# Down products as seven block products in place of eight: weight and activation quarters summed on the way, and one bank for the up products

## The reference

```python
def sq_relu_mlp(h, w_up, w_down):          # twice, D_FF = 4096
    return jnp.square(jax.nn.relu(h @ w_up)) @ w_down
# the FFN, D_FF_2 = 2816:  (silu(h @ w_gate) * (h @ w_up)) @ w_down
```

## Time and profile before

| | us |
|---|---|
| median of three executions (1137.82 to 1142.7) | 1138.17 |
| the profiled execution | 1141.42 |
| its span, first to last instruction | 1139.6 |
| TensorE busy in it | 1112.0 |
| VectorE busy | 707.6 |
| ScalarE busy | 583.6 |
| GpSimd busy | 142.6 |

### The profile page before, as it was taken

The page is one execution under the profiler, slowest core; times in us unless marked ns, Lnnn a source line. Parts: engine busy times, 40 slices in busy tenths (PEclk is TensorE's granted clock), DMA queues, the critical chain, the costliest instruction groups (busy, mean ns, idle before and its releaser), DMA issues.

```text
span 1139.6 us, 17781 instructions
## 1 busy us (share of the span) xinstructions
PE 1112.0 (98%) x7033; PEld 984.8 (86%) x7033; DVE 707.6 (62%) x997; ACT 583.6 (51%) x767; POOL 142.6 (13%) x105
## 2 busy tenths in 40 slices
PE   8899999999998999999999999999999999999997
PEld 7767888888887888888888999898899989999996
DVE  5764565565668646565656878566587566554554
ACT  5565544444579554444455546455555346443443
POOL 3543300000265240000030000000000011000001
PEclk9999999999999999999999999999999999999999
DMA  7917565555442236556545654436643545656552
GB/s 216 306 54 186 182 198 188 200 190 184 118 137 88 98 111 222 191 186 201 189 156 185 204 171 149 132 128 223 203 159 120 185 148 160 221 175 194 189 172 89
DMA packets 138782, 193.96 MB, mean 170 GB/s; under 512 B 7147, under 2 KB 112840, under 8 KB 138716
## 3 DMA queue, kind: packets, MB, share of 16 engines
q1 hardware_dynamic: 126796, 181.92, 48.4%
q10 hardware_dynamic: 11312, 11.05, 3.6%
q0 software_dynamic: 608, 0.08, 0.1%
HBM read 191.90 MB, written 6.37 MB: 174 GB/s over the span
## 4 chain that ended last, share of the span: by engine, by line
PE 83%; ACT 6%; DVE 5%; issue 2%; DMA 2%; POOL 0%; ACTq 0%; DVEq 0%; POOLq 0%
PE psum L548 20%; PE psum L549 20%; PE psum L550 20%; PE psum L709 11%; PE psum L710 5%; ACT arena L1552 3%; PE psum L637 2%; ACT whi L1566 2%; DVE wlo L2125 1%; DMA raw<-in_a_w_in 1%; PE psum L1264 1%; PE psum L668 1%; PE psum L1237 1%; DVE arena L2566 1%; DMA raw<-in_b_w_o 0%
## 5 line engine op out<-in xcount | busy, mean ns | idle before, releaser
L1566 ACT ACTIVATE whi<-raw 128x2048 fp32r<-128x2048 f32 (+2 forms) x174 | 325.9, 1875 | 255.5 <-PE psum L550 172.5
L2125 DVE TENSOR_TENSOR wlo<-raw,whi 128x2048 fp32r<-128x2048 f32 (+1 forms) x149 | 337.5, 2267 | 184.1 <-ACT whi L1566 183.2
L548 PE MATMUL psum<-xA,whi 128*128 128x256 f32 x840 | 239.8, 285 | 2.7 <-DVE wlo L2125 1.7
L549 PE MATMUL psum<-xA,whi 128*128 128x256 f32 x840 | 237.6, 283 | 0.0
L550 PE MATMUL psum<-xA,wlo 128*128 128x256 f32 x840 | 237.5, 283 | 0.0
L1535 POOL TENSOR_TENSOR wlo<-raw,whi 128x288 fp32r<-128x288 f32 (+3 forms) x56 | 112.6, 2037 | 793.8 <-ACT whi L1566 793.5
L709 PE MATMUL psum<-xA,whi 128*128 128x512 f32 x512 | 183.0, 400 | 0.0
L548 PEld LDWEIGHTS psum<-xA,whi 128*128 128x128 f32 x840 | 160.3, 191 | 6.0 <-DVE wlo L2125 3.2
L549 PEld LDWEIGHTS psum<-xA,whi 128*128 128x128 f32 x840 | 160.4, 191 | 0.7
L550 PEld LDWEIGHTS psum<-xA,wlo 128*128 128x128 f32 x840 | 160.4, 191 | 0.1
L548 PE MATMUL psum<-whi,xC 128*128 128x512 f32 (+1 forms) x384 | 149.2, 389 | 1.1 <-DVE xC L2439 1.1
(11 more groups left out here) (269 smaller groups left out, 1339.7 us busy)
## 6 DMA issues: line engine op xcount, KB each, us to landing
raw<-in_w_in SPq DMA_DIRECT2D x42, 1024.0 KB, 4.9
raw<-in_mlp_w_up SPq DMA_DIRECT2D x32, 1024.0 KB, 5.4
raw<-in_mlp_w_down SPq DMA_DIRECT2D x32, 1024.0 KB, 4.8
raw<-in_w_gate SPq DMA_DIRECT2D x11, 1024.0 KB, 5.1
raw<-in_w_up SPq DMA_DIRECT2D x11, 1024.0 KB, 5.2
raw<-in_w_down SPq DMA_DIRECT2D x11, 1024.0 KB, 4.8
raw<-in_a_w_in SPq DMA_DIRECT2D x6, 1024.0 KB, 7.1
raw<-in_a_w_o SPq DMA_DIRECT2D x4, 1024.0 KB, 4.7
```

The lines of the kernel that those rows point to most:

```text
L548: nc.tensor.matmul(out, lh, rh, start=start, stop=False, skip_group_check=skip)
L549: nc.tensor.matmul(out, lh, rl, start=False, stop=False, skip_group_check=skip)
L1566: nc.scalar.activation(whi[c % N_SPLIT][:, 0:n], raw[c % N_RAW][:, 0:n], ACT.Copy).then_inc(hi_sem, 1)
L2125: V.tensor_tensor(wlo[c % N_SPLIT][:, 0:n], raw[c % N_RAW][:, 0:n], f(whi[c % N_SPLIT][:, 0:n]), ALU.subtract).then_inc(lo_sem["dve"], 1)
```

## The change

The down product of a step is a 2 by 2 block matrix of activations (two token blocks, two hidden tiles) times a 2 by 2 block matrix of weights (two hidden tiles, two column halves), eight block products. The change computes it by a known scheme with seven, in which some factors are sums of quarters. Four sums of the weight quarters (`wsum`) are made on GpSimd in three instructions (1024, 512 and 512 elements per partition), and four sums of the activation quarters on VectorE in three (128, 256 and 128 elements). Of the chunk's own quarters three are used as they are, so high and low parts are made of 3 x 512 and of 4 x 512 elements: the high ones by ScalarE, the low part of the raw quarters by GpSimd (`raw_low`), that of the sums by VectorE (`sum_low`). The weight quarters' sums have one buffer for all steps; their high and low parts have two.

The seven products add to seven PSUM banks (1 to 7) through all steps but the last; at the end `seven_sums` on VectorE turns them into the four quarters of the output. The last step of each of the three stages keeps its eight products (`four_products`). That leaves one bank, 0, for the up products: in the MLP they change to the three-matmul form of 256 columns, 48 matmuls in place of 32, and ScalarE's copy and VectorE's addition and relu become one relu on ScalarE and a square on VectorE. In the FFN gate and up products use bank 0 in turn, with three of the seven products between them and four behind. Down chunks get two raw buffers of their own; all other chunks stay in the old ring. In the MLPs the norm's squares and scale move behind the first step. The first down chunk of each stage is loaded earlier, during the output product of the attention before.

The core of the diff (PE, POOL, ACT, DVE in this order; `count` turns a step's number into a semaphore value, in loops too):

```diff
+        wsum = area(14336, 4, 512)
+        raw_bufs = [raw[0][:, :], raw[1][:, :], down_raw[:, 0:SLOT], area(16384, SLOT)]
+        relu_buf = area(18432, 512)
+        hidden = down_raw[:, SLOT:SLOT + 1024]
...
+        seven = {"M1": (4, 1, 0), "M2": (3, 3, 2), "M3": (2, 7, 1), "M4": (1, 2, 6),
+                 "M5": (5, 4, 3), "M6": (6, 5, 5), "M7": (7, 6, 4)}
...
+            SEVEN = ("M1", "M6", "M7", "M5", "M2", "M3", "M4")
...
+            def seven_products(s, p, order, loop=None, start=False, closing=None, part=None):
+                if part in (None, 0):
+                    pe.wait_ge(down_low_raw, count(lambda x: sums_count(s, x)))
+                    pe.wait_ge(down_low_sum, count(lambda x: whole_count(s, x)))
+                    pe.wait_ge(hidden_low, count(lambda x: whole_count(s, x)))
+                wh, wl = [w[p % 2].rearrange("p (a n) -> p a n", n=512) for w in (down_hi, down_lo)]
+                xh, xl = [v[p % 2].rearrange("p (a n) -> p a n", n=P) for v in (hidden_hi, hidden_lo)]
+                for m in order:
+                    b, x, w = seven[m]
+                    ins = three(psum[:, b, :], xh[:, x, :], xl[:, x, :], wh[:, w, :], wl[:, w, :], start, True, True)
+                    if closing and b >= 4:
+                        close_bank(ins, f"{closing}.{m}")
+                if part in (None, 1):
+                    ins.then_inc(down_done, 1)
...
-                        out = psum[:, 4 + 2 * j2 + nt, :]
                         for k in range(KT):
                             if ready and nt == 0:
                                 ready(k)
-                            nc.tensor.matmul(out, hi[:, k, nt * P:nt * P + P], xA[:, :, k, :], start=k == 0, stop=False)
-                            ins = nc.tensor.matmul(out[:, 0:SEQ], lo[:, k, nt * P:nt * P + P], xA[:, 0, k, :],
-                                                   start=False, stop=k == KT - 1)
+                            ins = three(psum[:, b, nt * 256:nt * 256 + 256],
+                                        hi[:, k, nt * P:nt * P + P], lo[:, k, nt * P:nt * P + P],
+                                        xA[:, 0, k, :], xA[:, 1, k, :], k == 0, k == KT - 1)
...
+                up_step(0, 4, low[c0], None, late_tile(n))
+                up_step(1, 5, low[c0 + 1], None)
+                open_seven(n)
+                pe.wait_ge(relu_done, b0 + 2)
+                seven_products(i, 0, ("M2", "M3", "M4", "M6", "M7", "M1", "M5"), None, True)
...
+                with pe.Fori(0, 6) as r:
+                    for q in range(2):
+                        ps_ = [2 + 2 * y + q for y in range(6)]
+                        up_step(ps_[0] + 1, 0, along([low[index[f"mlp{i}.u{p + 1}"]] for p in ps_], r),
+                                along([b0 + p + 1 for p in ps_], r))
+                        seven_products(i, ps_[0], SEVEN, (ps_, r))
+                up_step(NM - 1, 0, low[index[f"mlp{i}.u{NM - 1}"]], b0 + NM - 1)
+                seven_products(i, NM - 2, SEVEN, None, False, n)
+                four_products(i, n)
...
+            def ffn_turn(p, loop=None, closing=None, cut_at=3):
+                wide_step(f"g{p + 1}", 0, count(lambda x: low[index[f"ffn.g{x + 1}"]]), (hidden_step, count(free_up)))
+                seven_products(2, p, SEVEN[:cut_at], loop, False, closing, 0)
+                wide_step(f"u{p + 1}", 0, count(lambda x: low[index[f"ffn.u{x + 1}"]]),
+                          (gate_scaled, count(lambda x: x + 2)))
+                seven_products(2, p, SEVEN[cut_at:], loop, False, closing, 1)
...
+            def weight_sums(s, p, loop=None):
+                c = down_chunk(s, p)
+                if p == 0:
+                    pool.wait_ge(*done[("A.oT3.hi", "B.oT3.hi", "C.m3.lo")[s]])
+                else:
+                    pool.wait_ge(down_low_sum, count(lambda x: whole_count(s, x - 1)))
+                pool.wait_ge(raw_sem[raw_of[c]], count(lambda x: landed[down_chunk(s, x)]))
+                b = raw_bufs[raw_of[c]].rearrange("p (a n) -> p a n", n=512)
+                T(wsum[:, 0:2, :], b[:, 0:1, :].to_broadcast([P, 2, 512]), b[:, 1:3, :], ALU.subtract).then_inc(down_sum, 1)
+                pool.wait_ge(down_sum, count(lambda x: 3 * sums_count(s, x) - 2))
+                T(wsum[:, 2, :], b[:, 1, :], wsum[:, 1, :], ALU.subtract).then_inc(down_sum, 1)
+                pool.wait_ge(down_sum, count(lambda x: 3 * sums_count(s, x) - 1))
+                T(wsum[:, 3, :], b[:, 3, :], wsum[:, 2, :], ALU.subtract).then_inc(down_sum, 1)
+            def raw_low(s, p, loop=None):
+                pool.wait_ge(down_sum, count(lambda x: 3 * sums_count(s, x)))
+                pool.wait_ge(down_high_raw, count(lambda x: whole_count(s, x)))
+                c = down_chunk(s, p)
+                T(down_lo[p % 2][:, 0:1536], raw_bufs[raw_of[c]][:, 512:SLOT], f(down_hi[p % 2][:, 0:1536]),
+                  ALU.subtract).then_inc(down_low_raw, 1)
...
+                for p in range(2):
+                    raw_low(s, p)
+                    weight_sums(s, p + 1)
...
+            def down_high(s, p, loop=None):
+                c = down_chunk(s, p)
+                act.wait_ge(raw_sem[raw_of[c]], count(lambda x: landed[down_chunk(s, x)]))
+                if p >= 2:
+                    act.wait_ge(down_done, count(lambda x: sums_count(s, x - 2)))
...
+                nc.scalar.activation(down_hi[p % 2][:, 0:1536], raw_bufs[raw_of[c]][:, 512:SLOT],
+                                     ACT.Copy).then_inc(down_high_raw, 1)
+                act.wait_ge(down_sum, count(lambda x: 3 * sums_count(s, x)))
+                nc.scalar.activation(down_hi[p % 2][:, 1536:3584], wsum.rearrange("p a n -> p (a n)"),
+                                     ACT.Copy).then_inc(down_high_sum, 1)
+            def hidden_copy(s, p, loop=None):
+                last = p == down_steps[s] - 1
+                act.wait_ge(hidden_step, count(lambda x: hidden_count(s, x, 1 if last else 4)))
+                if p >= 2:
+                    act.wait_ge(down_done, count(lambda x: sums_count(s, x - 2)))
+                v = slice(0, 512) if last else slice(P, 1024)
+                nc.scalar.activation(hidden_hi[p % 2][:, v], hidden[:, v], ACT.Copy).then_inc(hidden_high, 1)
...
+                def step(p, loop=None):
+                    relu(p, loop)
+                    down_high(i, p, loop)
+                    hidden_copy(i, p, loop)
+                    if loop:
+                        split_loop([index[f"mlp{i}.u{x + 2}"] for x in loop[0]], loop[1])
...
+            def hidden_sums(s, p, loop=None):
+                def step(k, ins):
+                    ins.then_inc(hidden_step, 1)
+                    at = [hidden_count(s, x, k) for x in (loop[0] if loop else (p,))]
+                    dve.wait_ge(hidden_step, along(at, loop[1]) if loop else at[0])
+                x = hidden.rearrange("p (a n) -> p a n", n=P)
+                step(2, V.tensor_tensor(x[:, 6, :], x[:, 0, :], x[:, 1, :], ALU.subtract))
+                step(3, V.tensor_tensor(x[:, 4:6, :], x[:, 0::6, :], x[:, 2:3, :].to_broadcast([P, 2, P]), ALU.add))
+                V.tensor_tensor(x[:, 7, :], x[:, 3, :], x[:, 5, :], ALU.subtract).then_inc(hidden_step, 1)
+            def sum_low(s, p, loop=None):
+                if p == down_steps[s] - 1:
+                    dve.wait_ge(down_high_raw, before(s) + p + 1)
+                    V.tensor_tensor(down_lo[p % 2][:, 0:SLOT], raw_bufs[N_RAW + p % 2], f(down_hi[p % 2][:, 0:SLOT]),
+                                    ALU.subtract).then_inc(down_low_sum, 1)
+                    return
+                at = [sums_count(s, x) for x in (loop[0] if loop else (p,))]
+                dve.wait_ge(down_high_sum, along(at, loop[1]) if loop else at[0])
+                V.tensor_tensor(down_lo[p % 2][:, 1536:3584], wsum.rearrange("p a n -> p (a n)"),
+                                f(down_hi[p % 2][:, 1536:3584]), ALU.subtract).then_inc(down_low_sum, 1)
+            def hidden_rest(s, p, loop=None):
+                at = [whole_count(s, x) for x in (loop[0] if loop else (p,))]
+                dve.wait_ge(hidden_high, along(at, loop[1]) if loop else at[0])
+                v = slice(0, 512) if p == down_steps[s] - 1 else slice(P, 1024)
+                V.tensor_tensor(hidden_lo[p % 2][:, v], hidden[:, v], f(hidden_hi[p % 2][:, v]),
+                                ALU.subtract).then_inc(hidden_low, 1)
+            def seven_sums(n):
+                def scaled(b, half, src, then=None):
+                    h = hres[:, b, 512 * half:512 * half + 512]
+                    run(V.scalar_tensor_tensor(h, src, late_scale[:, b:b + 1], h, ALU.mult, ALU.add), then)
+                dve.wait_ge(*read[f"{n}.M1"])
+                dve.wait_ge(*full[f"{n}.M6"])
+                run(V.tensor_tensor(wsum[:, 1, :], psum[:, 6, :], wsum[:, 0, :], ALU.add), read[f"{n}.M6"])
+                scaled(1, 1, wsum[:, 0, :])
+                dve.wait_ge(*full[f"{n}.M7"])
```

(30 more changed lines are left out.)

593 lines of the change are left out of this document (340 added, 253 removed).

## The result

The changed kernel takes 1277.57 us, the median of four executions (1273.8 to 1278.07), against 1139.68 for the kernel before in four (1137.82 to 1142.7): a ratio of 1.12, interval 1.1164 to 1.1236, so 138 us more. The forecast was 1256, within 1208 to 1305. The profiled execution has a span of 1276.3 us, 136.7 more than before.

What follows compares the result with a forecast made beforehand. The prediction took TensorE to bound the kernel before, and the SBUF port shared by VectorE and GpSimd the changed one. Two MLPs at +58 us and the FFN at +2 gave +118 on 1138.2: 1256 us, range 1208 to 1305.

Steps and rivals of the forecast that it cites:

- three small rows: Kernel before: small two-SBUF-input VectorE instructions meeting GpSimd's ended with it, one taking 1.05 us instead of 0.16.
- (a): Rival: long instructions don't exclude each other; TensorE sets steps of 10.55 and 16.31 us, total 1123 us; chance 0.12.
- (b): Rival: only VectorE waits, GpSimd goes on; MLP step about 12.5 us, total 1187 us; chance 0.07.
- The size of a step: MLP: VectorE's 7.34 and GpSimd's 8.45 us share one port, 15.8 us, taken as 15.2 (14.4 to 16.3).
- The overlap at the changes of holder: MLP step: about 8 holder changes save 0.1 us each, 0.8 off; four waits inside VectorE's run give 0.2 back.
- 14 intervals at the pace of the exclusion: Each MLP: fourteen intervals between seven products, each 15.2 - 11.1 = 4.1 us longer, +57.4 us.
- -2.3 for the last interval: Each MLP: the last port-bound interval has no next up weights to prepare, 2.3 us less.
- The start: Stage start: GpSimd's first down sums ahead of u1's low part could cost 0 to 4.9 us; taken as 0.
- The end of a stage: Behind the last step: VectorE's seven-product sums delay the first transposes, 3.0 us in each of three stages (0 to 5).
- The FFN: FFN: step stays 17.0 us (16.3 to 17.6); with 3 for the end and -1 for light last steps, +2 us.
- TensorE's idle time: MLP step: TensorE waits 4.6 us ahead of the seven products for the activations' low part, busy about 70%.
- (c): Rival: TensorE's clock falls in its new idle times and TensorE becomes late; 17 us per step, 1309 us; chance 0.07.

Runs made afterwards that it cites:

- e2: Changed kernel with GpSimd's four large instructions of a down step replaced by memsets, each behind an 8-element subtraction: 1158.34 us, 1.0156 of the kernel before.
- e9: Changed kernel with only the three sums of raw weight quarters moved to VectorE, their low part staying on GpSimd: 1228.77 us, 1.0773 of the kernel before.
- e3: Changed kernel with GpSimd's weight sums and raw low part of the down steps all done by VectorE: 1203.09 us, 1.056 of the kernel before.
- e5: Changed kernel with the additions of the seven products at each stage's end done on 8 columns in place of 512: 1268.71 us.
- e11: Mended change (sums mostly on VectorE, MLP square on ScalarE, better start), with VectorE's next-stage low part moved behind four PSUM-reading additions: 1136.15 us, 0.9959 of the kernel before.
- e4: Changed kernel with TensorE awaiting the second relu only before one product, and the norm's squares and scale behind step 1: 1275.59 us against 1277.57.
- e6: Changed kernel with the edits of e2, e4 and e5 together: 1131.11 us, 0.9917 of the kernel before.

## Why the forecast held, and where its terms were off

**The mechanism was right.** The forecast rested on three small rows and said that large instructions exclude each other too, on both sides. e2's rows and e9's show it directly, e3 and e9 as a dose. The Trainium skill's rule ("SBUF — State Buffer", § Who interferes with whom), with its exception for a GpSimd instruction that only writes, is what e2 shows: memset not held, 8-element subtraction held 1.05 us. Rivals (a) and (b) fall by the same rows: the 2048-element subtraction didn't keep its 2.29 us, and GpSimd's sum of 512 took 3.22, so GpSimd waits as well.

**The size of a step.** Forecast 15.2 (14.4 to 16.3), measured 14.73. The demand was right: VectorE's seven instructions beside no reading GpSimd in e2 take 7.4 us. The overlap at the changes of holder was put too low: 15.8 - 14.7 = 1.1 us and not 0.6. Seven holds at about 0.14 us make 1.0 of it. The low end of the step's range has a slip: 15.8 less eight times 0.2, with none back, is 14.2 and not 14.4; the measured step lies above both.

**The count of steps was wrong.** I charged 14 intervals at the pace of the exclusion. The first two are 12.49 and 10.65: VectorE and GpSimd had prepared ahead while TensorE waited. With the term "-2.3 for the last interval", which isn't seen (14.78), the 14 came to +57.4 - 2.3 = +55.1 by forecast and +44.4 by the trace.

**The edges were mis-sized, the other way.** The start was put at 0 (0 to 4.9) and costs 10.1 us per MLP: GpSimd's sums and VectorE's activation sums meet, and in front of the first seven products ScalarE's relu of step 1 stands behind the norm's squares (143.68), which TensorE waits for though one of the seven needs it. I had written that the norm's small operations, moved behind the first step, are needed only at its end, without asking who stood behind them. The end of a stage was put at 3.0 (0 to 5) and costs 6.6 and 7.5 in the MLPs, since GpSimd's low part for the next stage meets the additions: held additions are 3.25 us of the 6.6, and with additions of 8 columns 5.6 of the 7.5 stay (e5). So the MLP's +61 and +62 against +58 forecast are two errors, -11 and +14, that nearly cancel: that the MLP's total came out so close is luck, its step is not.

**The FFN.** The step was 17.0 by forecast and is 7.92 + 9.2 = 17.1 (mean of the eight from the second pair of intervals on): right. But the stage lost 11.0 and not 2: 3.9 ahead of its first seven products, 1.9 from TensorE's last matmul to the end of the span (7.75 to 9.66), 1.1 in its eight steps. The other 4 arise right behind the start. Of the seven products of a step the first three stand ahead of the up product, but in the first step all seven do, so the first interval has one product of 5.76 us and not two, and its matmuls need 10.55 us; it takes 15.59 (1097.56 to 1113.15). In it VectorE's two low parts meet GpSimd's sums and take 5.93 us, not 4.49 as in e3 (at 1063.18), and TensorE stands still inside the first seven products with three matmuls left:

```profile
1099.59 5.93 DVE L2341 TENSOR_TENSOR wlo<-raw,whi 128x2048 fp32r<-128x2048 f32 x2 [2.50 <-ACT whi L1728]
```

```profile
1106.18 0.49 PE L611 MATMUL psum<-down_split,xB 128*128 128x512 f32 x1 [2.65 <-DVE down_raw L3055]
```

Most of the rest of the 5 us goes with TensorE's granted clock, 0.80 from 1097.5 to 1106.1, behind a gap of 3.70 us. Ahead of that gap VectorE's sum of 128 elements takes 3.57 us (at 1089.72) beside GpSimd's 1536. So most of the FFN's 11 us comes from such meetings at its start, which the forecast put at nothing.

**TensorE's idle time.** Forecast 4.6 us per step and 70% busy. It stands still for 3.88 and 1.65 us in two neighbouring steps, 82% busy: of the slack of 14.7 - 10.65 = 4.1 us a mean of 2.7 is idle and 1.4 is lost to the granted clock, 0.92 over the stretch above, a mean of the 1.2 and the 2.4 GHz level: the first matmul behind the gap of 3.88 us shows 0.77 us, the one behind 1.65 us (at 226.74) 0.48. That is rival (c)'s premise without its result: TensorE still waits in each step, and with the clock at 1.00 the steps of e3 are set by VectorE.

**Rival (a)'s price was wrong** though it was not put to the test by the result. I gave 1123 us for the change without exclusion; e2 comes nearest to that kernel, and takes 1158. Its step is 10.65 as worked out (10.55), the rest are the edges. Its additions behind an MLP still meet GpSimd's low parts; but even with both of its MLP ends (16.2 and 17.3 us) as short as before (10.9) it would take about 1147 by this estimate. So without the exclusion too this kernel would probably have been slower than the one before, and the 0.11 for faster rested on a wrong price. (That 0.11 and the 0.02 for no change also add up to more than the 0.12 given to the rival.)

## What to carry to other kernels

Before giving an idle GpSimd work, list VectorE's instructions with both inputs in SBUF and add the two engines' times as if they were one engine; here that sum, less about 0.14 us for each hold, was the step, whatever the busy shares said. Put VectorE's PSUM-reading instructions beside GpSimd's (e11), and those with both inputs in SBUF elsewhere; an instruction of 8 elements pays the whole wait (e5). A scheme that saves matmuls must be priced with its first and last step: here 10 us at the start and 7 at the end of each MLP stand against 15 x 0.683 - 16 x 0.12 = 8.3 us of saved stream in it.

## What the runs showed that was not expected

- Holding doesn't depend on size in the sizes run here: two 8-element additions took 8.89 us beside GpSimd's two subtractions of 4.6 us each (e5), and an 8-element GpSimd subtraction 1.25 in place of 0.20 (e2).
- A held instruction ends about 0.14 us sooner behind its holder than it takes alone: with seven holds the step was 1.1 us below the sum of durations, with two it was the sum (13.02 against 13.0).
- Where two engines exclude each other, both look busy in the profile: 188.28 and 150.90 us of a 190.83 us stretch, for work that takes 7.4 and 8.45 us of a 14.7 us step.
- A better start is worth nothing while something else sets the pace (e4, 4.5 us gained and 0.8 kept) and is kept once TensorE does (e6).
